# Attention of two layers: scaling the result rows instead of the probabilities

## The reference, cut to what matters

```python
def one_block(q_blk):                    # 128 queries
    s = jnp.einsum('bqgrd,bkgd->bgrqk', q_blk, k) * scale
    p = jax.nn.softmax(s, axis=-1)
    return jnp.einsum('bgrqk,bkgd->bqgrd', p, v)
```

## Time and profile before

| what | us |
|---|---|
| median of 3 runs | 1841.16 (1838.09 to 1843.55) |
| the profiled execution | 1837.36 |
| its span in the profile | 1835.6 |
| PE busy (of the span) | 1747.3 (95%) |
| DVE busy | 1131.6 (62%) |
| ACT busy | 681.2 (37%) |
| POOL busy | 182.1 (10%) |
| units of layer 0 (PE, from the first turn of probabilities) | 221.4 to 346.9 |
| units of layer 1 | 1223.2 to 1363.9 |

### The profile page before, as it was taken

The page is one execution under the profiler, slowest core; times in us unless marked ns, Lnnn a source line. Parts: engine busy times, 40 slices in busy tenths (PEclk is TensorE's granted clock), DMA queues, the critical chain, the costliest instruction groups (busy, mean ns, idle before and its releaser), DMA issues.

```text
span 1835.6 us, 23669 instructions
## 1 busy us (share of the span) xinstructions
PE 1747.3 (95%) x9274; PEld 1468.2 (80%) x9274; DVE 1131.6 (62%) x1692; ACT 681.2 (37%) x1117; POOL 182.1 (10%) x200
## 2 busy tenths in 40 slices
PE   6999999999999999999999999789989899999998
PEld 4777899777888888887777888679977788888776
DVE  5776777687577666545353777877866644443554
ACT  4442366443412212123343433334445423222342
POOL 1176400001100000000000200011210200000000
PEclk9999999999999999999999999899999899999999
DMA  9433000130243444521121132100011132223221
GB/s 363 156 116 114 24 1 1 69 115 23 104 161 137 139 170 158 200 81 69 46 92 46 49 114 71 46 24 1 1 69 69 47 115 91 91 94 110 94 92 69
DMA packets 30994, 166.77 MB, mean 91 GB/s; under 512 B 4144, under 2 KB 4656, under 8 KB 16688
## 3 DMA queue, kind: packets, MB, share of 16 engines
q1 hardware_dynamic: 29024, 163.60, 24.6%
q10 hardware_dynamic: 1872, 1.82, 0.3%
HBM read 163.31 MB, written 2.10 MB: 90 GB/s over the span
## 4 chain that ended last, share of the span: by engine, by line
PE 83%; DVE 7%; issue 4%; ACT 3%; DVEq 1%; DMA 1%; POOL 1%; ACTq 0%; POOLq 0%; SPq 0%
PE PS L293 12%; PE PS L297 12%; PE PS L295 12%; PE PS L583 8%; PE PS L585 7%; PE PS L584 7%; PE PS L1086 5%; PE PS L320 3%; PE PS L322 3%; PE PS L321 3%; PE PS L1071 2%; DVE w_lo L282 2%; ACT w_hi L276 1%; DVE pre_tmp_pre L487 1%; PE PS L597 1%
## 5 line engine op out<-in xcount | busy, mean ns | idle before, releaser
L293 PE MATMUL PS<-HT,w_hi 128*128 128x512 f32 (+1 forms) x1232 | 378.4, 355 | 10.8 <-DVE HT L493 5.0
L297 PE MATMUL PS<-HT,w_lo 128*128 128x512 f32 (+1 forms) x1232 | 370.8, 349 | 0.0
L295 PE MATMUL PS<-HT,w_hi 128*128 128x512 f32 (+1 forms) x1232 | 370.1, 349 | 0.0
L282 DVE TENSOR_TENSOR w_lo<-w_raw,w_hi 128x2048 fp32r<-128x2048 f32 x103 | 237.6, 2308 | 157.2 <-ACT w_hi L276 153.0
L583 PE MATMUL PS<-w_hi,a_ring 128*128 128x512 f32 x680 | 274.5, 404 | 15.1 <-DVE a_ring L659 5.6
L584 PE MATMUL PS<-w_lo,a_ring 128*128 128x512 f32 x680 | 265.8, 391 | 0.0
L293 PEld LDWEIGHTS PS<-HT,w_hi 128*128 128x128 f32 x1232 | 206.9, 189 | 52.3 <-issue 7.0
L276 ACT ACTIVATE w_hi<-w_raw 128x2048 fp32r<-128x2048 f32 x103 | 196.1, 1905 | 136.0 <-PEq L617 69.3
L297 PEld LDWEIGHTS PS<-HT,w_lo 128*128 128x128 f32 x1232 | 206.8, 189 | 30.9
L295 PEld LDWEIGHTS PS<-HT,w_hi 128*128 128x128 f32 x1232 | 206.8, 189 | 30.8
L958 DVE SCALAR_TENSOR_TENSOR yb<-PS,cws,yb 128x511 f32<-128x511 f32 (+1 forms) x132 | 83.2, 658 | 170.0 <-ACTq L924 166.2
(11 more groups left out here) (307 smaller groups left out, 2603.1 us busy)
## 6 DMA issues: line engine op xcount, KB each, us to landing
w_raw<-wpack SPq DMA_DIRECT2D x103, 1024.0 KB, 4.8
m_raw<-modu SPq DMA_DIRECT2D x80, 512.0 KB, 4.3
mod_raw<-modw SPq DMA_DIRECT2D x8, 1024.0 KB, 12.2
X<-x SPq DMA_DIRECT2D x1, 2048.0 KB, 8.6
out<-X SPq DMA_DIRECT2D x4, 512.0 KB, 2.6
X<-ctx SPq DMA_DIRECT2D x1, 1024.0 KB, 10.8
alnb<-aln ACTq DMA_DIRECT2D x1, 512.0 KB, 4.3
csn<-rope_ev ACTq DMA_DIRECT2D x1, 256.0 KB, 2.6
```

What stands on the lines that cost most here:

```text
L282: nc.vector.tensor_tensor(w_lo[r][:, :], w_raw[r][:, :], w_hi[r][:, :].bitcast(F32), ALU.subtract).then_inc(wl_ready, 1)
L293: nc.tensor.matmul(o, wh, xh, start=start, stop=False)
L295: nc.tensor.matmul(o, wh, xl, start=False, stop=False)
L297: last = nc.tensor.matmul(o, wl, xh, start=False, stop=stop)
```

## The change

The probabilities are turned as they come out of the exponential. In the values product the roles are exchanged: the turned probabilities stand in the array and V streams, one group of matmuls for each query tile, so that the result is queries by features. DVE multiplies that result (128 numbers of a row) by the reciprocal row sum into a new tile `O_q`, PE turns it by one transposition for each query tile into another part of bank 7, and DVE copies it to `cat` as before.

```diff
-        rsum = const("rsum", [P, 2, 2])
+        rsum = const("rsum", [P, 3, 2])
+        O_q = {False: at("O_q_ev", ..., [P, 2 * P]), True: at("O_q_od", ..., [P, P])}
 # PE
+            def out_turn(u):
+                pe.wait_ge(S("heads", "on"), units_before(odd) + u + 1)
+                for i in range(U[u][2]):
+                    last = nc.tensor.transpose(PS[:, 7, (2 + i) * P:(3 + i) * P], O_q[odd][:, i * P:(i + 1) * P], ident[:, :])
+                last.then_inc(S("heads", "turned"), 1)
             for u, (h, t, w, nk, k0) in enumerate(U):
-                pe.wait_ge(S(st, "p"), u + 1)
+                pe.wait_ge(S(st, "exp"), u + 1)
                 ...
                 last.then_inc(S(st, "ptr"), 1)
+                if u >= 1:
+                    out_turn(u - 1)
                 if u + 2 < len(U):
                     scores(u + 2)
                 ...
                 pe.wait_ge(S(st, "pT"), u + 1)
                 if u >= 1:
                     pe.wait_ge(S(st, "ocopy"), u)
                 ...
-                for j in range(nk):
-                    last = nc.tensor.matmul(PS[:, 7, 0:w * P], V[:, k0 + j, c:c + P], PT[u % 2][:, j * w * P:(j + 1) * w * P], ...)
+                for i in range(w):
+                    for j in range(nk):
+                        last = nc.tensor.matmul(PS[:, 7, i * P:(i + 1) * P], PT[u % 2][:, (j * w + i) * P:(j * w + i + 1) * P],
+                                                V[:, k0 + j, c:c + P], start=j == 0, stop=j == nk - 1)
                 last.then_inc(S(st, "o"), 1)
                 extra(u)
+            out_turn(len(U) - 1)
 # DVE
-            def normalise(u): ...      # reciprocal, then the probabilities times it, signals "p"
+            def normalised(u):
+                dve.wait_ge(S(st, "exp"), u + 1)
+                w, sm = U[u][2], rsum[:, u % 3, 0:U[u][2]]
+                nc.vector.reciprocal(sm, sm)
+                dve.drain()
+                dve.wait_ge(S(st, "o"), u + 1)
+                for i in range(w):
+                    last = nc.vector.tensor_scalar(O_q[odd][:, i * P:(i + 1) * P], PS[:, 7, i * P:(i + 1) * P], sm[:, i:i + 1],
+                                                   None, ALU.mult)
+                last.then_inc(S("heads", "on"), 1)
+            def copied(u):
+                dve.wait_ge(S("heads", "turned"), units_before(odd) + u + 1)
+                if u == 0 and not odd:
+                    dve.wait_ge(S("gate", "gated"), NT)
+                nc.vector.tensor_copy(cat[:, cat0 + h, t * P:(t + w) * P], PS[:, 7, 2 * P:(2 + w) * P]).then_inc(S(st, "ocopy"), 1)
             maxima(0)
             maxima(1)
             if not odd:
                 q_low(dve, 2)
-            normalise(0)
-            for u, (h, t, w, nk, k0) in enumerate(U):
-                if u + 1 < len(U):
-                    normalise(u + 1)
+            for u in range(len(U)):
+                if u >= 1:
+                    copied(u - 1)
                 if u + 2 < len(U):
                     maxima(u + 2)
                 if u + 3 < len(U) and not odd:
                     q_low(dve, u + 3)
-                (wait for "o", copy of u)
+                normalised(u)
                 extra(u)
+            copied(len(U) - 1)
```

More of the change, by code:

```diff
@@ L194, in build @@
         qNl = [at(f"qNl{i}", R_MOD + (14 + i) * 512, [P, P], F32R) for i in range(2)]
+        O_q = {False: at("O_q_ev", R_GM + 2 * KIB, [P, 2 * P]), True: at("O_q_od", R_A + 24 * KIB + 4 * 4 * (LAT + 2 * HALO), [P, P])}
         PTo = [at(f"PTo{i}", R_RAW1 + 3 * i * KIB, [P, TOK]) for i in range(2)]
@@ L1016, in q_low, with units_before @@
                                     ALU.subtract).then_inc(S("eva", "qTl"), 1)
+        def units_before(odd):
+            return len(units(False)) if odd else 0
         def attn_pe(pe, st, odd, U, lead=lambda: None, extra=lambda u: None):
@@ L1083, in attn_pe @@
                 V = Vod if odd else (V32 if u < 4 * LT else Vev)
-                for j in range(nk):
-                    c = h * P if odd else (h // 4) * P
-                    last = nc.tensor.matmul(PS[:, 7, 0:w * P], V[:, k0 + j, c:c + P], PT[u % 2][:, j * w * P:(j + 1) * w * P],
-                                            start=j == 0, stop=j == nk - 1)
+                c = h * P if odd else (h // 4) * P
+                for i in range(w):
+                    for j in range(nk):
+                        last = nc.tensor.matmul(PS[:, 7, i * P:(i + 1) * P], PT[u % 2][:, (j * w + i) * P:(j * w + i + 1) * P],
+                                                V[:, k0 + j, c:c + P], start=j == 0, stop=j == nk - 1)
                 last.then_inc(S(st, "o"), 1)
                 extra(u)
+            out_turn(len(U) - 1)
         def attn_act(act, st, odd, U, scale, extra=lambda u: None):
@@ L1102, in exps @@
                                                 bias=rmax[:, u % 2, i:i + 1], scale=scale,
-                                                accum_out=rsum[:, u % 2, i:i + 1])
+                                                accum_out=rsum[:, u % 3, i:i + 1])
                 last.then_inc(S(st, "exp"), 1)
@@ L1119, in attn_dve @@
         def attn_dve(dve, st, odd, U, scale, cat, extra):
-            Pb, cat0 = (Pod, 0) if odd else (Pe, 4)
+            cat0 = 0 if odd else 4
             def maxima(u):
```

9 lines of the change are left out of this document (3 added, 6 removed).

## The result

| | before | after |
|---|---|---|
| median of 4 runs each, us | 1840.24 (1838.09 to 1843.55) | 1855.81 (1853.99 to 1857.36) |
| the profiled execution | 1837.36 | 1853.99 |
| its span | 1835.6 | 1852.2 |
| PE busy | 1747.3, x9274 | 1762.1, x9386 |
| DVE busy | 1131.6 | 1109.2 |

The ratio is 1.0083, 95% interval 1.0064 to 1.0101: the change costs 15.3 us (11.8 to 18.6), 0.8%. The forecast was +12.2. The page's first part shows what was exchanged for what. DVE gave up 22 us of work. PE took on 112 more instructions: 80 transpositions of the result, and 32 because the values products of the context units are cut in two.

A forecast was written before the change was run, and what follows sets the result against it. The prediction took PE to bound both attention stages. Layer 0's terms summed to +7.7 us and layer 1's to +4.5, together +12.2 on the median of 1841.2, giving 1853.4 us, range 1844 to 1864.

The forecast's parts named there:

- Roles exchanged at nothing: Values products: exchanging the sides costs 0 in latent units, 0.1 us at most in context units, where PE waits anyway.
- A transposition at 0.11 us, with no gap to hide in: Every latent unit, on PE: one added transposition costs 0.11 us, as PE has no gap for it.
- The hand-over: Layer 0 latent units: PE stalls 0.08 us for the scaling; with the transposition 0.20 a unit taken, +6.0 us.
- Context units: Layer 0: the new wait for two scalings lengthens the period from 2.86 to 3.29 us, +2.6 us over six periods.
- End of layer 0: Output projection's first load waits for scalings and transpositions, +1.14 us; last values product about 0.35 more; +1.5 us.
- Start of layer 0: First turn no longer waits for normalising; POOL's gating then sets unit 1's values product at 225.6; -2.4 us.
- Start of layer 1: The first turn can follow the exponential, 0.9 us sooner, part of it at half clock: -0.6 us.
- `extra` ahead of the copy: Layer 1: values products wait for copies now behind `extra`, 0.3 us in units 8, 12, 16, 20; together +2.0 us.
- (A): Both layers: only the transposition costs, all waits are covered, starts gain their most; +3.9 us, about 1845; chance 0.13.
- (B): Every unit: DVE and PE hand over in series; +22 us, 1863, latent period 3.55 or more; chance 0.18.
- (C): Layer 0: the normalising loop is the true bound, so removing it lets PE run closer; about 1836; chance 0.04.
- (D): Attention stages: transpositions don't count for the clock gate, so the clock falls; ten falls add 17 us, 1870; chance 0.02.

The follow-up runs named there:

- again: The changed kernel run once more with nothing altered; median 1854.3 us, ratio 1.0076 to the kernel before.
- before_again: The kernel before the change, run once more with nothing altered; median 1843.4 us, ratio 1.0008.
- no_turn: Changed kernel without the result's transposition and second copy, DVE scaling straight into `cat` (output no longer the model's); median 1835.52 us, ratio 0.9963 to the kernel before.
- turned_twice: Changed kernel with every transposition of the result done twice into the same place; median 1861.42 us, ratio 1.0110 to the kernel before.
- turn_after_one: Changed kernel with the result's turn behind the first score matmul of unit u+2 instead of ahead of it; median 1848.22 us, ratio 1.0034 to before.
- copy_first: Changed kernel with `extra` behind the copy into `cat` on DVE instead of ahead of it; median 1848.68 us, ratio 1.0063 to the kernel before.
- first_unit_only: Kernel before, with the new way given only to the first unit of each layer's attention; median 1838.21 us, ratio 0.9977 to the kernel before.
- first_unit_later_copy: New way in each layer's first unit only, with DVE's normalising of unit 2 moved ahead of unit 0's copy; median 1837.97 us, ratio 0.9979 to before.
- late_turn: Changed kernel with the result's turn behind three (layer 1: five) score matmuls of unit u+2; median 1857.82 us, ratio 1.0096 to the kernel before.

## Why the prediction was right

The total: +12.2 forecast, 15.3 (11.8 to 18.6) measured. Term by term, from the starts of the values products in the two first traces; layer 0 ends with the first load of the output projection (354.25 against 346.85 in the earlier trace rows, 7.4 us):

| term | forecast | measured |
|---|---|---|
| layer 0, start | -2.4 | -2.7 |
| layer 0, latent units | +6.0 | +5.3 |
| layer 0, context units and end | +4.1 | +4.8 |
| layer 1, start | -0.6 | -2.2; with low clock, as in `again`, about -0.6 |
| layer 1, turns | +3.3 | +3.1 |
| layer 1, `extra` ahead of the copy | +2.0 | +5.0 |
| layer 1, end | -0.2 | -0.4 |

These terms add up to 12.2 forecast and 12.9 measured. The two profiled executions differ by 16.6; the rest of that lies outside the stages, 3.6 us of it at two places where `before_again` lost 0.9 and 1.8 as well. The interval of the medians takes in the 12.9. Two terms lie outside their own ranges: the start of layer 1 and its `extra`, which I had put at 0.5 to 4.

**Roles exchanged at nothing:** right, `no_turn`. **A transposition at 0.11 us, with no gap to hide in:** the price is right, `turned_twice` and layer 1's plain periods show it. The gap was there: in layer 0 PE waited 0.05 us a unit for ACT's copy into `PTe`, which the 90.00 of 90.00 in the earlier trace rows didn't show.

**The hand-over.** The sum gave 0.08 us of stall; the mean period of after shows 0.07 over the bare 0.11. I took 0.20 a unit in place of the 0.19 of that sum, and 0.18 came. But that 0.07 is made of two terms: by `turn_after_one` and by the starts of the loads the stall is 0.10 to 0.11 (0.01 of it from unit 7), and the wait for ACT, which is gone, gives 0.05 back. The mechanism was right, and its size came out because two small errors have opposite signs: the stall is larger than 0.08, in part since the scaling takes 0.35 and not 0.29, and the wait for ACT wasn't in my sum. I also missed the stop of DVE in unit 7, which reaches PE now.

**Context units:** 3.29 forecast, 3.27 measured in the plain ones. The nearest row had been the copy of 128 columns; two scalings took 0.61 and not 0.50, while the turns overlapped more than I took.

**End of layer 0.** The mechanism was incomplete. `part_lo`, 0.95 us of DVE, is also an `extra` and stands ahead of the copy in units 36 and 37. I had it in layer 1 and forgot it here.

**Start of layer 0.** POOL ended at 224.72 instead of 225.24, 7.96 us instead of 8.52 for its gating, since the normalising steps no longer stand beside it: two of its six operations took 1.60 us beside them, and neither of the two takes more than 1.27 now. By the rule of the Trainium skill that the prediction named, POOL had to finish sooner; the trace agrees. The clock did more than I said. It fell at this place in both traces of before, after an idle stretch of 3.19 us on PE, and in none of the ten others, where that stretch is 1.33. I had written that POOL sets the end either way. From its first turn to the values product of unit 1 PE took 6.62 us in before (221.37 to 227.99), while POOL had been done at 225.24. With the same fall it would come to that product at about 219.56 + 6.62 + 0.11 = 226.3 now, an estimate from these rows, and not at 225.25. So about 1.0 of the 2.7 us is the clock's.

**Start of layer 1.** Here the clock decides. The idle stretch went from 3.80 to 2.90 us. The clock fell behind it in both traces of before and in six of the ten others. The first trace of after is one of the four without a fall, and so its start is 2.2 us shorter. Its six transpositions take 0.88 us, not the 1.54 of the earlier trace rows; so they do in the other traces, `before_again` included (0.88 to 0.90), because there the fall comes only behind them. These are the windows of after and of `again` at the same work, two us apart:

```profile
1230.00:1238.00 8.00, 7.40 (x49) 6.67 (x50) 3.77 (x9) 6.59 (x12) 0.74 (x2) 1.00 0.00 1
```

```profile
1232.00:1240.00 8.00, 7.34 (x40) 6.61 (x41) 3.48 (x8) 5.29 (x9) 0.46 (x1) 0.79 0.00 0
```

My -0.6 was right for a start with low clock.

**`extra` ahead of the copy.** Right in kind and place, as `copy_first` shows, and too small by a factor of 2.5. For unit 8 the copy was to start 3.83 us after the unit's values product; it started at 3.89. I allowed 0.34 from there to the next product, and it took 0.43: PE's product starts 0.15 behind the end of the copy, not 0.05 as in the earlier trace rows. That makes 0.46 in place of 0.30. The larger part are terms I didn't have. The unit behind each of these stalls loses 0.08; I put that down to DVE, which is behind and so makes its scaling late. Unit 25 loses 0.97 and not 0.2, and unit 1 0.77 and not 0.36.

**The rivals.** (A) is excluded by time. (B) had the right place in layer 1, where the `extra` units lost even more than its 4 us; in layer 0 the period stayed at 3.38, far from its 3.55. (C) fell with `no_turn`: without the normalising step the latent period is 3.19 as before. It was right in that the records overstate PE a little, by the 0.05 us a unit, half of the 0.1 that it asked for. (D): no window in the middle of a stage shows a clock under 1.00, with 80 or, in `turned_twice`, 160 more transpositions. The rule of the Trainium skill that stood behind it ("TensorE: Matmul & The Clock Gate", Part 4) may hold for transpositions by themselves, which no run here shows; among this many products it had no effect.

So the forecast was right in its mechanisms for the transposition, the hand-over and `extra`, and in its sum also by luck, because two errors have opposite signs: layer 1's start came 1.6 us shorter, its `extra` units 3.0 us longer. With the clock of `again` the first error is gone, and the two stages together are +14.4.

## What to carry to other kernels

Work taken off an engine that is not the bound buys nothing: 17.7 us less of DVE's work in `no_turn`'s window left the period as it was. Work put on the bound is paid for, 0.11 us for each transposition in `turned_twice`. But 90.00 of 90.00 us busy doesn't say that the engine never waits: the starts of its loads showed 0.05 us a unit, which is why the first transposition cost 0.08 in `turn_after_one`. When a value makes a round trip (PE, DVE, PE, DVE), look at both hand-overs and at all that stands between them in the queue of the slower engine; one score product ahead of the transposition halved layer 0's loss, three made it larger than it was. And where a change wins only at the start of a loop, give it to the first unit alone.

## What the runs showed of the hardware

- The same DVE instruction, 768 columns from SBUF to SBUF, takes 0.62 us or 1.28 to 1.51 beside POOL. It isn't slowed evenly. In `first_unit_only` it starts 0.08 us ahead of POOL's next operation and takes its 0.62, and that operation takes 1.67 instead of 1.26. In `first_unit_later_copy` it starts within one of POOL's operations and takes 1.51, and POOL's next one, a copy, 1.80 instead of 1.46:

```profile
227.16 1.51 DVE L1178 TENSOR_SCALAR Pe<-Pe,rsum 128x768 f32<-128x768 f32 x1
...
228.19 1.80 POOL L1359 COPY Vev<-V 128x1536 f32<-128x1536 f32 x1
```

  It looks as if one waits for the other to end. The Trainium skill says so ("Trainium Architecture — The Big Picture", What this means for kernel authors): the ports that DVE and POOL share are locked by one of them, not divided. These rows agree.
- The granted clock can fall at a place in one execution of a program and not in the next. Behind the 2.90 us for which PE is idle ahead of layer 1's units it fell in six of ten traces (in `again` but not in after, which are the same kernel). So a difference of a microsecond or two between two traces has to be read stage by stage, and a second trace of the same kernel is the cheapest control.
- From the end of a DVE operation to the PE load that waits for it, it took 0.05 us (the context units' transposition), 0.06 (the latent units') or 0.12 (the values product behind a late copy, `late_turn` and unit 8 alike). One price for all of them was too simple.
